# Splitting the streamed weights two blocks at a time in a TensorE-bound kernel of four model layers

## The chip, the cores and the metric

The kernel runs on one core of a Trainium2 chip. The metric is the device time of one execution in microseconds (us).

## The reference

Four transformer layers work on 256 tokens of width 2048, in float32. The first two have three mixers side by side (a causal depthwise convolution over 31 tokens, a gated linear recurrence with 6 heads, retention with 6 heads) and a feed-forward with squared ReLU of width 8192, each followed by a layer norm of the residual sum. The third has neighbourhood attention, a gated delta rule in both directions and attention on a memory; the fourth has differential attention and attention on the memory. Cut to what the time goes into:

```python
proj = einsum('btd,de->bte', x, w_in[l])              # 2048 x 7168
...                                                   # mixers on parts of proj
x = layer_norm(ALPHA * x + mix @ w_out[l], ...)       # 2048 x 2048
f = square(relu(x @ w_ff1[l]))                        # 2048 x 8192
x = layer_norm(ALPHA * x + f @ w_ff2[l], ...)         # 8192 x 2048
...                                                   # twice, then
h = rmsnorm(x, ln_g); proj = h @ w_in                 # and out: x + mix @ w_out, twice
```

The results have to be near float32, so each product is made of three: weights and activations are split into a high part, which TensorE takes as float32r, and the difference to it, the low part, and hi·hi + lo·hi + hi·lo is summed.

## The kernel before

**Units and blocks.** All large products run through one weight stream. A unit is 512 output columns of a weight matrix over 2048 rows; it has 8 blocks of 256 rows (BLOCKS = 8), each 128 partitions x 2 x 512 elements, 512 KB. There are 140 units, 1120 blocks. The program numbers blocks of a stage with c and keeps block c in ring buffer j = c % 8 of `raw` (as loaded), `w_hi` and `w_lo`; `w_lo` lies in the same memory as `raw`. `ps_unit` has two buffers of sums, for units in turn.

**The four engines of the stream.** SyncE (`sp_unit`, L243) waits with `block_done` until block c-8 has been used, then loads block c and raises `raw_ready[j]` by 16. ScalarE (`act_split`, L251) waits for `raw_ready[j]` and copies `raw` to `w_hi` (L255), raising `hi_ready` by 1. VectorE (`dve_split`, L258) waits for `hi_ready` and subtracts (L262), raising `lo_ready`. TensorE (`pe_block`, L265) waits for `lo_ready` to reach c + 1 and issues 12 matmuls (L279 to L281: 2 row groups x 2 token tiles x 3 products), the last of which raises `block_done`.

**Order around the splits.** Each engine runs a list of instructions written out by hand. ScalarE and VectorE are 6 blocks ahead of TensorE (AHEAD = 6): in the place that belongs to TensorE's block c they split block c + 6, and between those places stands their other work: taking sums out of `ps_unit` (L697, L712), the transposed activations (`act_turn_bank`, `dve_turn_bank`, L766 and L779), and the mixers. `split_units` (L624) is the plain loop, `Meanwhile` (L651) hands out splits one at a time between the mixers' steps, and `act_feed_forward` and `dve_feed_forward` have their own loops. In the very first unit of the program the six blocks 0 to 5 are split one by one between the first transposes (L3702, L3751).

**The seams.** Where a layer norm ends one stage and the next stage multiplies its result, the two are interleaved. TensorE (`pe_seam_last`, `pe_seam_first`) works through the last unit's second half token tile by token tile, so that the norm of tile 0 can start, and then takes the next unit: blocks 0 to 3 for tile 0, blocks 0 to 3 for tile 1, blocks 4 to 7 for both, with eight transposing steps (L307, four matmuls each, a bank of `ps_mix` per step) between them: banks 2 and 3 after blocks 2 and 3 of tile 0, 4 and 5 in tile 1, 6 and 7 after block 4. It waits for the low part of block 2 and of block 3 when it takes them for tile 0. ScalarE's part is `act_seam` (L353), VectorE's is `dve_seam` (L374): statistics of a tile, then `norm.columns` (for LayerNorm L438, a reciprocal L443, L446), which write x 512 columns at a time, `dve_seam_bank` (L371), the low part of a transposed bank, and at three places a split: block 3 (L408), and blocks 4 and 5 inside the loop of L412:

```python
    dve_split(dve, k, b0, c0 + SEAM - 1)
    norm.columns(dve, k, 1, (0, 1))
    dve_seam_bank(dve, k, 2)
    dve_seam_bank(dve, k, 3)
    for c in (2, 3):
        norm.columns(dve, k, None, (c,))
        dve_split(dve, k, b0, c0 + SEAM + c - 2)
        for t in range(TT):
            dve_seam_bank(dve, k, 2 * c + t)
```

There are four seams: two with layer norm in layer 1 (after w_out, and after the feed-forward), one in layer 2 (after w_out), and one with RMS norm between layers 3 and 4.

Of the kernel before, what the change touches and what calls it, by code (L numbers as in the profile page):

```python
# [7 lines left out]
F32 = mybir.dt.float32  # L8
F32R = mybir.dt.float32r
I32 = mybir.dt.int32  # L10
ACT = mybir.ActivationFunctionType
ALU = mybir.AluOpType
# [21 lines left out]
BLOCKS = 8  # L34
# [216 lines left out]
def act_split(act, k, b0, c):  # L251

    j = c % BLOCKS
    act.wait_ge(k.raw_ready[j], b0 * 2 + 16 * (c // BLOCKS + 1))
    k.nc.scalar.activation(k.w_hi[:, j], k.raw[:, j], ACT.Copy).then_inc(k.hi_ready, 1)  # L255


def dve_split(dve, k, b0, c):  # L258

    j = c % BLOCKS  # L260
    dve.wait_ge(k.hi_ready, b0 + (c + 1))
    k.nc.vector.tensor_tensor(k.w_lo[:, j], k.raw[:, j], k.w_hi[:, j].bitcast(F32), ALU.subtract).then_inc(k.lo_ready, 1)  # L262


def pe_block(pe, k, b0, c, hi, lo, tiles=range(TT), at=None):  # L265
# [358 lines left out]
def split_units(eng, k, who, split, units, take=None, last=False):  # L624


    first = k.block0[who]
    k.block0[who] += units * BLOCKS
    pairs = units // 2

    def pair(b0, i, ending):
        for s in range(2):
            for c in range(AHEAD, AHEAD + BLOCKS):
                if take and c == AHEAD + BLOCKS - 1:
                    take(b0, s, i)
                if not (ending and s == 1 and c >= BLOCKS):
                    split(eng, k, b0, s * BLOCKS + c)

    loops = pairs - 1 if last else pairs
    if loops:  # L640
        with eng.Fori(0, loops) as i:
            pair(i * (2 * BLOCKS) + first, i, False)
    if last:
        pair(first + loops * 2 * BLOCKS, loops, True)
# [49 lines left out]
def act_take_proj(act, k, column=0):  # L694
    def take(b0, s, i):
        wait_unit(act, k, b0, s)
        k.nc.scalar.activation(k.proj[:, :, bass.ds(i * (2 * NC) + (column + s * NC), NC)], k.ps_unit[:, s],  # L697
                               ACT.Copy).then_inc(k.evacuated, BLOCKS)
    return take
# [524 lines left out]
def act_conv(act, k, l, run):  # L1224

    a = k.nc.scalar
    act.wait_ge(*run.evacuated(0))
    cg = k.proj[:, :, CG:CG + CONV_C]
    a.activation(cg, cg, ACT.Sigmoid).then_inc(*k.conv_gate.up())
    run(28)  # L1230
    act_hgrn_gates(act, k, l, run)
    upto(run, 40 + LATE * l)
    act.wait_ge(*k.conv_var.next("act"))
    a.activation(k.conv_rstd[:], k.conv_mv[:, :, 1], ACT.Sqrt, bias=k.eps[:, 0:1]).then_inc(*k.conv_root.up())
    run(2)
    act.wait_ge(*k.conv_linear.next("act"))
    ca = k.proj[:, :, CA:CA + CONV_C]
    a.activation(ca, ca, ACT.Silu).then_inc(*k.conv_done.up())
# [478 lines left out]
def act_take_first(act, k):  # L1717


    take_proj = act_take_proj(act, k, HQ)  # L1720

    def take(b0, s, i):
        if HQ + (2 * i + s) * NC < RG_LAST:
            return take_proj(b0, s, i)
        wait_unit(act, k, b0, s)
        k.nc.scalar.activation(k.proj[:, :, RG_LAST:RG_LAST + NC], k.ps_unit[:, s], ACT.Silu).then_inc(k.evacuated, BLOCKS)
    return take
# [344 lines left out]
def act_gate_split(act, k):  # L2072
    act.wait_ge(*k.gw_in.next("act", 16))
    k.nc.scalar.activation(k.gw_hi[:], k.gw_raw[:], ACT.Copy).then_inc(*k.gw_hi_ready.up())
# [1549 lines left out]
def two_blocks_kernel(nc, dram, out):  # L3624
    k = set_up(nc, dram, out)
# [4 lines left out]
    with nc.Block() as block:  # L3630
# [69 lines left out]
        @block.scalar  # L3700
        def _(act):
            for c in range(AHEAD):  # L3702
                act_split(act, k, 0, c)
                act_turn_bank(act, k, c)
            for g in range(AHEAD, BLOCKS):
                act_turn_bank(act, k, g)
            act.wait_ge(*k.eps_set.next("act"))
            for l in range(DEPTH):
                split_units(act, k, "act", act_split, CONV_UNITS, act_take_proj(act, k))
                run = Meanwhile(act, k, "act", act_split, IN_UNITS - CONV_UNITS, act_take_first(act, k))  # L3710
                act_conv(act, k, l, run)
                if l == 0:
                    act_positions(act, k)
                act_hgrn(act, k, l, run)
                act_retention(act, k, l, run)
                act_out_units(act, k, act_ln_root(act, k), late={AHEAD + 1: (4,), AHEAD + 3: (5, 6, 7)})
                if l < DEPTH - 1:
                    act_feed_forward(act, k, l, root=act_ln_root(act, k))
                else:
                    act_feed_forward(act, k, l, between=act_memory(act, k))  # L3720

            run = Meanwhile(act, k, "act", act_split, MEM_UNITS, act_take_memory(act, k))
            run(1)
            act_layer_norm(act, k)
            run(10)
            act.wait_ge(*k.normed.next("act", BLOCKS))
            act_rms(act, k, k.x, k.normed_x)
            run(6)
            act_gate_split(act, k)
            run.rest()  # L3730
            act_turn(act, k)
            split_units(act, k, "act", act_split, DELTA_UNITS, act_take_proj(act, k, DQ))
            run = Meanwhile(act, k, "act", act_split, IN_UNITS - DELTA_UNITS, act_take_columns(act, k, EVEN_COLUMNS))
            act_even_inputs(act, k, run)
            act_even_attention(act, k)
            act_delta(act, k, run)
            act_out_units(act, k, act_rms_root(act, k))
            split_units(act, k, "act", act_split, IN_UNITS - ODD_UNITS, act_take_proj(act, k, MQ))
            act_odd_attention(act, k, Meanwhile(act, k, "act", act_split, ODD_UNITS, act_take_odd(act, k)))
            act_odd_out(act, k)  # L3740

        @block.vector
        def _(dve):
            dve.sem_inc(k.evacuated, 2 * BLOCKS)
            dve.sem_inc(k.f_lo_ready, 2)
            dve.wait_ge(*k.consts_in.next("dve", 16))
            for g in range(BLOCKS):
                if g % 2 == 0:
                    dve.wait_ge(*k.x_in[g // 2].next("dve", 16))
                    dve.sem_inc(*k.turn_source.up(2))  # L3750
                if g < AHEAD:  # L3751
                    dve_split(dve, k, 0, g)
                dve_turn_bank(dve, k, g)
            for l in range(DEPTH):
                split_units(dve, k, "dve", dve_split, CONV_UNITS)
                run = Meanwhile(dve, k, "dve", dve_split, IN_UNITS - CONV_UNITS)
                if l == 0:
                    dve_positions(dve, k)
                dve_conv(dve, k, l, run)
                dve_hgrn(dve, k, l, run)  # L3760
                dve_retention(dve, k, l, run)
                dve_out_units(dve, k, LayerNorm(ALPHA), late={AHEAD + 2: (5, 6, 7)})
                if l < DEPTH - 1:
                    dve_feed_forward(dve, k, l, norm=LayerNorm(None))
                else:
                    dve_feed_forward(dve, k, l, between=dve_memory(dve, k))
            run = Meanwhile(dve, k, "dve", dve_split, MEM_UNITS)
            dve_layer_norm(dve, k, FF_GROUPS * OUT_UNITS, k.normed, run)
            run(14 - run.done)
            dve.wait_ge(*k.row_in.next("dve", 16))  # L3770
            dve_rms(dve, k, k.x, k.normed_x, k.gain, run)
            run(20 - run.done)
            dve_gate_split(dve, k)
            run.rest()
            dve_turn(dve, k)
            split_units(dve, k, "dve", dve_split, DELTA_UNITS)
            dve_gate_rows(dve, k)
            run = Meanwhile(dve, k, "dve", dve_split, IN_UNITS - DELTA_UNITS)
            dve_even_inputs(dve, k, run)
            dve_even_attention(dve, k)  # L3780
            dve_delta(dve, k, run)
            dve_out_units(dve, k, RootMeanSquare())
            split_units(dve, k, "dve", dve_split, IN_UNITS - ODD_UNITS)
            dve_odd_attention(dve, k, Meanwhile(dve, k, "dve", dve_split, ODD_UNITS))
            dve_odd_out(dve, k)
# [57 lines left out]
```

## Time and profile before

| | |
|---|---|
| median of 3 runs | 3428.34 us (3423.22 to 3429.39) |
| the profiled execution, its own time | 3427.86 us |
| its span | 3426.1 us |
| TensorE (PE) busy | 3379.8 us, 99% |
| VectorE (DVE) busy | 2187.7 us, 64% |
| ScalarE (ACT) busy | 1592.4 us, 46% |
| high copies, L255 | 1120, 1174.4 us |
| low differences, L262 | 1120, 1373.6 us |
| mean granted TensorE clock | 0.999 |

The span is what the profiler saw of the execution from its first to its last instruction; busy times are unions over it. An instruction of VectorE or ScalarE begins a little before the one ahead of it ends, so start-to-start is shorter than the duration. Matmuls overlap too: one of 512 columns is shown as 0.39 us, and the next starts about 0.23 us after it.

### The profile page before, as it was taken

To read this page: it belongs to the slowest core of one execution; us is meant where nothing else is said; L and a number is where in the kernel's file an instruction comes from. 1 tells how busy PE (TensorE), PEld (TensorE's weight loads), DVE (VectorE), ACT (ScalarE), POOL (GpSimd) and SP (SyncE) were. 2 spreads that over 40 slices of the span, in tenths; PEclk is the share of its full clock that TensorE was granted. 3 is DMA by queue.
4 is the path that set the end of the run, shared out by engine and by line. 5 is a ranking of instruction groups with operands and counts; after the bars stand their busy time and mean duration, and the time that the engine had idled before them with its cause. 6 is when DMAs were issued, how large, how long until landed. Compare 5 with 4: busy or idle time off the path is not lost.

```text
span 3426.1 us, 42773 instructions
## 1 busy us (share of the span) xinstructions
PE 3379.8 (99%) x16007; PEld 2819.9 (82%) x16007; DVE 2187.7 (64%) x2543; ACT 1592.4 (46%) x1968; POOL 366.7 (11%) x394
## 2 busy tenths in 40 slices
PE   8999999999999999999999999999999999999999
PEld 7888878888888787888788888888888889888887
DVE  5976666555555678865665656667446676656664
ACT  4554444444434346444444444344445643365563
POOL 0035001010101001520101010100000152000100
PEclk9999999999999999999999999999999999999999
DMA  7645666666666665556767666766666701565644
GB/s 235 191 141 167 198 207 213 198 212 199 212 200 213 186 197 171 146 156 206 258 205 212 199 208 203 206 197 207 186 178 175 205 31 52 187 189 172 181 133 166
DMA packets 333642, 633.82 MB, mean 185 GB/s; under 512 B 27561, under 2 KB 37801, under 8 KB 331803
## 3 DMA queue, kind: packets, MB, share of 16 engines
q1 hardware_dynamic: 313120, 595.93, 57.4%
q0 software_dynamic: 11136, 29.18, 2.8%
q10 hardware_dynamic: 9216, 6.30, 0.6%
q8 instruction: 123, 2.02, 0.2%
q14 instruction: 47, 0.39, 0.0%
HBM read 612.44 MB, written 2.10 MB: 179 GB/s over the span
## 4 chain that ended last, share of the span: by engine, by line
PE 91%; DVE 4%; ACT 3%; DMA 1%; issue 1%; ACTq 0%; SPq 0%; DVEq 0%
PE ps_unit L279 28%; PE ps_unit L281 27%; PE ps_unit L280 27%; PE ps_mix L2980 2%; PE ps_mix L1362 1%; DVE sb_w_lo L262 1%; ACT sb_w_hi L255 1%; DMA sb_raw<-in_w_in_dram 1%; PE ps_mix L737 0%; PE ps_mix L307 0%; DVE sb_x L438 0%; DMA sb_raw<-in_w_ff_dram 0%; PE ps_mix L3410 0%; DMA sb_raw<-in_e_w_in_dram 0%; PE ps_mix L3430 0%
## 5 line engine op out<-in xcount | busy, mean ns | idle before, releaser
L262 DVE TENSOR_TENSOR sb_w_lo<-sb_raw,sb_w_hi 128x1024 fp32r<-128x1024 f32 x1120 | 1373.6, 1241 | 996.2 <-ACT sb_w_hi L255 990.9
L255 ACT ACTIVATE sb_w_hi<-sb_raw 128x1024 fp32r<-128x1024 f32 x1120 | 1174.4, 1059 | 1450.8 <-DMA sb_raw<-in_w_ff_dram 530.4
L279 PE MATMUL ps_unit<-sb_w_hi,sb_a_hi 128*128 128x512 f32 x3456 | 1360.5, 394 | 7.5 <-DVE sb_a_lo L779 4.8
L281 PE MATMUL ps_unit<-sb_w_hi,sb_a_lo 128*128 128x512 f32 x3456 | 1347.9, 390 | 0.0
L280 PE MATMUL ps_unit<-sb_w_lo,sb_a_hi 128*128 128x512 f32 x3456 | 1347.0, 390 | 0.0
L279 PEld LDWEIGHTS ps_unit<-sb_w_hi,sb_a_hi 128*128 128x128 f32 x3456 | 650.2, 188 | 144.7 <-DVE sb_a_lo L779 5.4
L281 PEld LDWEIGHTS ps_unit<-sb_w_hi,sb_a_lo 128*128 128x128 f32 x3456 | 649.9, 188 | 136.8
L280 PEld LDWEIGHTS ps_unit<-sb_w_lo,sb_a_hi 128*128 128x128 f32 x3456 | 650.6, 188 | 131.7
L279 PE MATMUL ps_unit<-sb_w_hi,sb_f_hi 128*128 128x512 f32 x1024 | 399.2, 390 | 0.0
L281 PE MATMUL ps_unit<-sb_w_hi,sb_f_lo 128*128 128x512 f32 x1024 | 398.5, 389 | 0.0
L280 PE MATMUL ps_unit<-sb_w_lo,sb_f_hi 128*128 128x512 f32 x1024 | 398.4, 389 | 0.0
L281 PEld LDWEIGHTS ps_unit<-sb_w_hi,sb_f_lo 128*128 128x128 f32 x1024 | 192.3, 188 | 40.1
L280 PEld LDWEIGHTS ps_unit<-sb_w_lo,sb_f_hi 128*128 128x128 f32 x1024 | 192.3, 188 | 39.6
L279 PEld LDWEIGHTS ps_unit<-sb_w_hi,sb_f_hi 128*128 128x128 f32 x1024 | 192.3, 188 | 39.6
L1000 POOL DMA_DIRECT2D sb_f_in<-sb_f_out x192 | 94.0, 497 | 1105.5 <-DVE sb_f_out L1053 1102.7
L1288 DVE SCALAR_TENSOR_TENSOR sb_conv_y<-sb_conv_u,sb_conv_w,sb_conv_y 128x255 f32<-128x255 f32 (+29 forms) x240 | 96.9, 474 | 0.1
L712 DVE TENSOR_TENSOR sb_x<-sb_x,ps_unit 128x1024 f32<-128x1024 f32 (+1 forms) x43 | 49.3, 1147 | 70.0 <-PE ps_unit L281 69.7
L697 ACT ACTIVATE sb_proj<-ps_unit 128x1024 f32<-128x1024 f32 (+1 forms) x45 | 46.1, 1025 | 79.0 <-PE ps_unit L281 79.0
L1454 POOL TENSOR_TENSOR sb_h_d<-sb_h_cum 128x768 f32<-128x768 f32 x16 | 37.1, 2318 | 339.0 <-DVE sb_h_cum L1525 251.8
L723 DVE BATCH_NORM_STATS2 sb_stats<-sb_x 128x6 f32<-128x512 f32 x80 | 51.5, 686 | 1.4
L975 ACT ACTIVATE sb_f_hi<-sb_f_out 128x512 fp32r<-128x512 f32 x64 | 36.9, 624 | 28.9 <-DVE sb_f_out L1024 28.7
L350 ACT ACTIVATE sb_a_hi<-ps_mix 128x512 fp32r<-128x512 f32 x32 | 18.7, 598 | 64.0 <-PE ps_mix L307 64.0
(474 smaller groups left out, 1972.5 us busy)
## 6 DMA issues: line engine op xcount, KB each, us to landing
sb_raw<-in_w_ff_dram SPq DMA_DIRECT2D x512, 512.0 KB, 3.8
sb_raw<-in_w_in_dram SPq DMA_DIRECT2D x224, 512.0 KB, 3.7
sb_raw<-in_e_w_in_dram SPq DMA_DIRECT2D x112, 512.0 KB, 3.5
sb_raw<-in_o_w_in_dram SPq DMA_DIRECT2D x112, 512.0 KB, 4.5
sb_raw<-in_w_out_dram SPq DMA_DIRECT2D x64, 512.0 KB, 4.0
sb_raw<-in_e_w_out_dram SPq DMA_DIRECT2D x32, 512.0 KB, 4.4
sb_raw<-in_o_w_out_dram SPq DMA_DIRECT2D x32, 512.0 KB, 3.6
sb_raw<-in_e_w_mem_kv_dram SPq DMA_DIRECT2D x16, 512.0 KB, 4.5
```

Source lines behind the costliest of these rows:

```text
L255: k.nc.scalar.activation(k.w_hi[:, j], k.raw[:, j], ACT.Copy).then_inc(k.hi_ready, 1)
L262: k.nc.vector.tensor_tensor(k.w_lo[:, j], k.raw[:, j], k.w_hi[:, j].bitcast(F32), ALU.subtract).then_inc(k.lo_ready, 1)
L279: k.nc.tensor.matmul(acc, hi[:, kt, tokens], w_hi, start=kt == 0, stop=False)
L280: k.nc.tensor.matmul(acc, hi[:, kt, tokens], w_lo, start=False, stop=False)
L281: last = k.nc.tensor.matmul(acc, lo[:, kt, tokens], w_hi, start=False, stop=kt == KT - 1)
L697: k.nc.scalar.activation(k.proj[:, :, bass.ds(i * (2 * NC) + (column + s * NC), NC)], k.ps_unit[:, s], ACT.Copy).then_inc(k.evacuated, BLOCKS)
L712: return k.nc.vector.tensor_tensor(x, x, out, ALU.add)
L723: last = k.nc.vector.bn_stats(k.stats[:, t, bass.ds(chunk, 1), :].rearrange("p c s -> p (c s)"), k.x[:, t, cols])
L1000: pool.dma_start(*moved_square(k, u, n)).then_inc(k.f_moved_pool[u % 2], 16)
L1288: ins = v.scalar_tensor_tensor(y, u, w, y, ALU.mult, ALU.add)
L1454: g.tensor_tensor(d[:, :, 0, :], middle, c[:, :, 0, :], ALU.subtract)
L2980: last = tensor.matmul(out[:, x, :], left(n), right[:, n, :], start=True, stop=True)
```

## The change

`act_split` and `dve_split` do nothing for an even buffer j. For an odd j they wait for both blocks, j-1 and j, and treat them in one instruction of 2048 elements per partition (the two ring buffers are next to each other), raising `hi_ready` and `lo_ready` by 2. So an even block is split in the place that belonged to the odd one behind it. The loops that call them are as before. The six single blocks at the start get functions of their own, which are the old ones. TensorE's and SyncE's programs are unchanged, and so are all numbers that are waited for.

```diff
 def act_split(act, k, b0, c):
 
     j = c % BLOCKS
+    if j % 2 == 0:
+        return
+    act.wait_ge(k.raw_ready[j - 1], b0 * 2 + 16 * (c // BLOCKS + 1))
     act.wait_ge(k.raw_ready[j], b0 * 2 + 16 * (c // BLOCKS + 1))
-    k.nc.scalar.activation(k.w_hi[:, j], k.raw[:, j], ACT.Copy).then_inc(k.hi_ready, 1)
+    k.nc.scalar.activation(k.w_hi[:, j - 1:j + 1], k.raw[:, j - 1:j + 1], ACT.Copy).then_inc(k.hi_ready, 2)
+
+
+def act_split_one(act, k, c):
+
+    act.wait_ge(k.raw_ready[c], 16)
+    k.nc.scalar.activation(k.w_hi[:, c], k.raw[:, c], ACT.Copy).then_inc(k.hi_ready, 1)
 
 
 def dve_split(dve, k, b0, c):
 
     j = c % BLOCKS
+    if j % 2 == 0:
+        return
+    pair = slice(j - 1, j + 1)
     dve.wait_ge(k.hi_ready, b0 + (c + 1))
-    k.nc.vector.tensor_tensor(k.w_lo[:, j], k.raw[:, j], k.w_hi[:, j].bitcast(F32), ALU.subtract).then_inc(k.lo_ready, 1)
+    k.nc.vector.tensor_tensor(k.w_lo[:, pair], k.raw[:, pair], k.w_hi[:, pair].bitcast(F32), ALU.subtract)\
+        .then_inc(k.lo_ready, 2)
+
+
+def dve_split_one(dve, k, c):
+
+    dve.wait_ge(k.hi_ready, c + 1)
+    k.nc.vector.tensor_tensor(k.w_lo[:, c], k.raw[:, c], k.w_hi[:, c].bitcast(F32), ALU.subtract).then_inc(k.lo_ready, 1)
...
             for c in range(AHEAD):
-                act_split(act, k, 0, c)
+                act_split_one(act, k, c)
                 act_turn_bank(act, k, c)
...
                 if g < AHEAD:
-                    dve_split(dve, k, 0, g)
+                    dve_split_one(dve, k, g)
                 dve_turn_bank(dve, k, g)
```

What moves in a seam, in the order of each engine's own instructions. VectorE in the first layer-norm seam, from the end of columns 2 on, before (L446 writes x, L262 is a split, L371 the low part of a bank, L438 the first half of columns 3):

```order
L446 SCALAR_TENSOR_TENSOR sb_x<-sb_x,sb_rstd,sb_shift 128x512 [waits dve_step]
L446 SCALAR_TENSOR_TENSOR sb_x<-sb_x,sb_rstd,sb_shift 128x512
L262 TENSOR_TENSOR sb_w_lo<-sb_raw,sb_w_hi 128x1024 [waits hi_ready]
L371 TENSOR_TENSOR sb_a_lo<-ps_mix,sb_a_hi 128x4x128 [waits turn_hi] x2
L438 SCALAR_TENSOR_TENSOR sb_x<-sb_x,sb_mv,sb_gain 128x512 [waits aggregated]
L438 SCALAR_TENSOR_TENSOR sb_x<-sb_x,sb_mv,sb_gain 128x512
L446 SCALAR_TENSOR_TENSOR sb_x<-sb_x,sb_rstd,sb_shift 128x512 [waits dve_step]
L446 SCALAR_TENSOR_TENSOR sb_x<-sb_x,sb_rstd,sb_shift 128x512
L262 TENSOR_TENSOR sb_w_lo<-sb_raw,sb_w_hi 128x1024 [waits hi_ready]
L371 TENSOR_TENSOR sb_a_lo<-ps_mix,sb_a_hi 128x4x128 [waits turn_hi] x2
```

and the same place in the changed kernel, whose lines have other numbers (L465 for L446, L390 for L371, L457 for L438, L274 for L262):

```order
L465 SCALAR_TENSOR_TENSOR sb_x<-sb_x,sb_rstd,sb_shift 128x512 [waits dve_step]
L465 SCALAR_TENSOR_TENSOR sb_x<-sb_x,sb_rstd,sb_shift 128x512
L390 TENSOR_TENSOR sb_a_lo<-ps_mix,sb_a_hi 128x4x128 [waits turn_hi] x2
L457 SCALAR_TENSOR_TENSOR sb_x<-sb_x,sb_mv,sb_gain 128x512 [waits aggregated]
L457 SCALAR_TENSOR_TENSOR sb_x<-sb_x,sb_mv,sb_gain 128x512
L465 SCALAR_TENSOR_TENSOR sb_x<-sb_x,sb_rstd,sb_shift 128x512 [waits dve_step]
L465 SCALAR_TENSOR_TENSOR sb_x<-sb_x,sb_rstd,sb_shift 128x512
L274 TENSOR_TENSOR sb_w_lo<-sb_raw,sb_w_hi 128x2048 [waits hi_ready]
L390 TENSOR_TENSOR sb_a_lo<-ps_mix,sb_a_hi 128x4x128 [waits turn_hi] x2
```

Block 4's split has moved from ahead of banks 4 and 5 and columns 3 to behind them.

ScalarE in the same seam, before (`turned` tells that TensorE has transposed a bank; `raw_ready4` is buffer 4's load):

```order
L350 ACTIVATE sb_a_hi<-ps_mix 128x4x128 [waits turned] x2
L255 ACTIVATE sb_w_hi<-sb_raw 128x1024 [waits raw_ready4]
L255 ACTIVATE sb_w_hi<-sb_raw 128x1024 [waits raw_ready5]
L350 ACTIVATE sb_a_hi<-ps_mix 128x4x128 [waits turned] x4
L255 ACTIVATE sb_w_hi<-sb_raw 128x1024 [waits raw_ready6]
L255 ACTIVATE sb_w_hi<-sb_raw 128x1024 [waits raw_ready7]
```

and now (L369 for L350, L258 for L255):

```order
L369 ACTIVATE sb_a_hi<-ps_mix 128x4x128 [waits turned] x2
L258 ACTIVATE sb_w_hi<-sb_raw 128x2048 [waits raw_ready5,raw_ready4]
L369 ACTIVATE sb_a_hi<-ps_mix 128x4x128 [waits turned] x4
L258 ACTIVATE sb_w_hi<-sb_raw 128x2048 [waits raw_ready7,raw_ready6]
L258 ACTIVATE sb_w_hi<-sb_raw 128x2048 [waits raw_ready1,raw_ready0]
```

Each pair stands where its two single copies stood together.

## Rows read from the trace of the kernel before

**Rows 1.** The page: busy time of each engine, share of the span, instructions.
```profile
PE 3379.8 (99%) x16007; PEld 2819.9 (82%) x16007; DVE 2187.7 (64%) x2543; ACT 1592.4 (46%) x1968; POOL 366.7 (11%) x394
```

**Rows 2.** Windows: stretch, then PE, PEld, DVE, ACT, POOL busy, clock, DMA, GB/s.
```profile
560.00:600.00 40.00, 40.00 (x178) 33.14 (x177) 21.52 (x21) 16.82 (x17) 2.93 (x6) 1.00 0.67 210
```

**Rows 3.** The page: loads of weight blocks, count, KB, us from issue to landing.
```profile
sb_raw<-in_w_ff_dram SPq DMA_DIRECT2D x512, 512.0 KB, 3.8
```

**Rows 4.** Groups by form: count, busy us, mean ns of one, idle before.
```profile
L262 DVE TENSOR_TENSOR sb_w_lo<-sb_raw,sb_w_hi 128x1024 fp32r<-128x1024 f32 x1120 | 1373.6, 1241 | 996.2 <-ACT sb_w_hi L255 990.9
L255 ACT ACTIVATE sb_w_hi<-sb_raw 128x1024 fp32r<-128x1024 f32 x1120 | 1174.4, 1059 | 1450.8 <-DMA sb_raw<-in_w_ff_dram 530.4 <-DMA sb_raw<-in_w_in_dram 257.0 <-issue 216.9
L1952 ACT ACTIVATE sb_normed_x<-sb_x 128x2048 f32<-128x2048 f32 x2 | 3.8, 1903 | 0.0
L2311 DVE TENSOR_TENSOR sb_proj<-sb_proj,sb_head_ss 128x1536 f32<-128x1536 f32 x8 | 13.9, 1755 | 0.1
```

**Rows 5.** Groups by form, TensorE: the transposes of the seams.
```profile
L307 PE MATMUL ps_mix<-sb_square,sb_x 128*128 128x128 f32 x96 | 14.4, 277 | 6.5 <-DVE sb_x L446 6.5
L307 PE MATMUL ps_mix<-sb_square,sb_normed_x 128*128 128x128 f32 x32 | 4.7, 274 | 0.2 <-DVE sb_normed_x L476 0.2
```

**Rows 6.** Timeline of VectorE, first seam: start us, us, instruction, idle before.
```profile
467.27 1.21 DVE L262 TENSOR_TENSOR sb_w_lo<-sb_raw,sb_w_hi 128x1024 fp32r<-128x1024 f32 x1
...
477.26 1.22 DVE L262 TENSOR_TENSOR sb_w_lo<-sb_raw,sb_w_hi 128x1024 fp32r<-128x1024 f32 x1
...
481.93 1.41 DVE L446 SCALAR_TENSOR_TENSOR sb_x<-sb_x,sb_rstd,sb_shift 128x512 f32<-128x512 f32 x2
483.26 1.22 DVE L262 TENSOR_TENSOR sb_w_lo<-sb_raw,sb_w_hi 128x1024 fp32r<-128x1024 f32 x1
...
486.20 8.04 DVE L262 TENSOR_TENSOR sb_w_lo<-sb_raw,sb_w_hi 128x1024 fp32r<-128x1024 f32 x7
```

**Rows 7.** Timeline of ScalarE, first seam: the splits from block 6 on.
```profile
485.11 6.75 ACT L255 ACTIVATE sb_w_hi<-sb_raw 128x1024 fp32r<-128x1024 f32 x7
```

**Rows 8.** Timeline of TensorE, first seam: transposes, first matmuls of blocks 4, 5, 6.
```profile
470.73 0.66 PE L307 MATMUL ps_mix<-sb_square,sb_x 128*128 128x128 f32 x4 [1.19 <-DVE sb_x L446]
...
480.62 0.50 PE L279 MATMUL ps_unit<-sb_w_hi,sb_a_hi 128*128 128x512 f32 x1
...
484.53 0.50 PE L279 MATMUL ps_unit<-sb_w_hi,sb_a_hi 128*128 128x512 f32 x1
...
487.58 0.47 PE L279 MATMUL ps_unit<-sb_w_hi,sb_a_hi 128*128 128x512 f32 x1
```

**Rows 9.** Waits of TensorE: waited for, us in total, times, longest.
```profile
PE ps_mix L3418 <- DVE sb_o_att_e L3539: 3.2, 1, 3.2
...
PE ps_mix L1642 <- DVE sb_r_rstd L1737: 2.8, 2, 1.7
PE ps_mix L1263 <- DVE sb_conv_y L1288: 2.4, 1, 2.4
PE ps_unit L279 <- DVE sb_w_lo L262: 1.8, 4, 0.9
...
PE ps_mix L1371 <- DVE sb_h_s L1550: 1.4, 1, 1.4
```

**Rows 10.** Windows of 1 us after two waits: TensorE busy, granted clock.
```profile
171.00:172.00 1.00, 1.00 (x4) 0.66 0.07 18
172.00:173.00 1.00, 1.00 (x4) 0.50 0.00 0
...
174.00:175.00 1.00, 1.00 (x4) 0.63 0.00 0
...
3317.00:3318.00 1.00, 1.00 (x7) 1.00 0.02 8
```

**Rows 11.** Timeline of VectorE: splits in the mixers.
```profile
167.08 1.23 DVE L262 TENSOR_TENSOR sb_w_lo<-sb_raw,sb_w_hi 128x1024 fp32r<-128x1024 f32 x1 [1.03 <-ACT sb_w_hi L255]
...
2905.57 2.36 DVE L262 TENSOR_TENSOR sb_w_lo<-sb_raw,sb_w_hi 128x1024 fp32r<-128x1024 f32 x2
...
3313.72 1.23 DVE L262 TENSOR_TENSOR sb_w_lo<-sb_raw,sb_w_hi 128x1024 fp32r<-128x1024 f32 x1 [4.06 <-ACT sb_w_hi L255]
```

## The prediction

> **What bounds the kernel now.** I read the page's busy times first: TensorE is busy 3379.8 of 3426.1 us, so 46.3 us are idle; VectorE is busy 64% of the span, ScalarE 46% [rows 1]. Less work on those two is worth at most what TensorE waits for them. Then the windows: in 40 us of feed-forward TensorE issues 178 matmuls of 512 columns [rows 2]; a block has 12, so it takes one block each 40 / 178 x 12 = 2.70 us.
>
> Then the weight ring. Eight buffers; the load of block c starts when block c-8 is done, so the load, ScalarE's high copy and VectorE's low difference must be through in 7 blocks, 18.9 us. Now they take 3.8 us [rows 3] + 1.06 + 1.24 [rows 4] = 6.1 us. 12.8 us are to spare, and TensorE's own waits name the low half with 1.8 us in all [rows 9]. The exceptions are the seams: the places where a layer norm's last tile is finished while TensorE already works on the next unit. There both splits stand between steps of the norm, and the timelines of one seam (467 to 488 us) are the second thing to read [rows 6 to 8].
>
> **The change in the steady ring.** 1120 blocks less 6 single ones make 557 pairs. ScalarE: its row of 2048 elements takes 1.90 us [rows 4], against 1.06 for 1024. VectorE: 1024 elements 1.24, 1536 elements 1.755 us [rows 4], hence about 1.03 us per 1024 more than what one takes: a pair takes about 2.29 us. The seven back to back splits start (8.04 - 1.22) / 6 = 1.137 us apart [rows 6], so a pair frees 2 x 1.137 - 2.205 = 0.07 us of VectorE, 39 us in all, none of it on TensorE's path. The pair waits for the second load, one block later: 2.7 + 3.8 + 1.90 + 2.29 = 10.7 us of 18.9. 8.2 us remain: cost nothing, as long as a load lands in under 12 us.
>
> The Trainium skill says more for the change: "VectorE: DVE Perf Modes", section on the TRN2 errata, has every instruction pay a fixed latency between instructions, once for a large tile and again for each small one; by its figure of about 151 cycles at 0.96 GHz a pair would save 157 ns, 88 us over 557 pairs (an estimate by that page). The splits of [rows 6] overlap by 0.085 us, so the trace gives less than half of that.
>
> **The seams.** There are four: 96 + 32 transposes at L307, 32 each [rows 5]. In each the even block of a pair loses its own place and gets that of the odd one, while TensorE takes it as early as before. Numbers of the first seam; blocks 2 to 7 of the unit:
> - Pair 2+3, in the place of block 3's split, 467.27 us [rows 6]: VectorE is 2.205 - 1.137 = 1.07 us longer, and the columns of x behind it, for which TensorE waits 1.19 us before its transposes at 470.73 [rows 8], come 1.07 us later. **+1.07**. With no slack there all behind it moves.
> - Pair 4+5. Block 4 was split at 477.26, block 5 at 483.26 [rows 6]. The pair stands at 483.26. The 1.14 us that leave at 477.26 don't help: the next two low halves wait for TensorE's transposes. So 483.26 + 1.07 + 2.29 = 486.62, and TensorE begins block 4 at 486.67 where it began at 480.62 [rows 8]: +6.05, or **+4.98** on top. The pause is about 5 us.
> - Pair 6+7. After block 4 come the transposes of the last two banks; ScalarE copies them out and right behind that splits block 6, at 485.11 [rows 7]. This chain follows block 4, so the pair begins at 485.11 + 6.05 = 491.16, its high copy ends at 493.06, its low half at 493.09 + 2.29 = 495.38, TensorE's matmul follows 0.16 us behind it, as now, at 495.54 instead of 487.58 [rows 8]: +7.96, **+1.9** on top. Block 5 follows block 4 by 3.91 us (484.53 less 480.62 [rows 8]), begins at 490.58 and is done 2.6 us later, so a second pause of 2.3 us stands before block 6.
> Later blocks have 3 us and more to spare. Sum 7.95 us a seam; 4 x 7.95 = **+31.8 us**. (The RMS seam has other steps of the same length.) Bounds: 1.07 + 4.98 alone, if the last chain hides (24 us), to 9 us each (36).
>
> **The clock.** Pauses of this length can cost twice. After the wait of 2.4 us for sb_conv_y the windows show a granted clock of 0.50, that is 1.2 GHz, with 4 matmuls a us in place of 6, from 171.3 to 174.7 us (0.66 and 0.63 in the slices at its ends); after the wait of 3.2 us for sb_o_att_e it stays at 1.00, 2.4 GHz [rows 9, 10]. The slow stretch of 3.4 us costs half of that, 1.7 us. The changed seam has a pause of 5 us and one of 2.3 us in a row; I take one stretch a seam: 4 x 1.7 = **+6.8 us**, bounds 0 and 13.6. [...] Of the waits in the rows one had the fall and one not, so the sum keeps 6.8.
>
> **The mixers.** Where VectorE had an even split, waiting for ScalarE, just ahead of a step that TensorE waits for, that split is gone. At 167.08 us the split waited 1.03 us and took 1.23 [rows 11] ahead of the last taps: the 2.4 us wait shrinks by some 1.2 (the pair before costs 1 us), and its slow stretch goes, 1.7. At 3313.72 the split of an even block waited 4.06 us [rows 11] ahead of sb_o_att_e: 3.0 of the 3.2 us go. The waits for sb_h_s (1.4) and sb_r_rstd (2.8, two times) [rows 9] have an even split ahead as well: 4.0 of their 4.2. Sum -10.9. On the other side, where TensorE takes an even block just after its split: at 2905.57 both splits follow each other [rows 11] with TensorE taking the first 0.12 us after it, so a pair costs (1.90 - 1.06) + (2.29 - 1.22) = 1.9 us; I count seven more places where a pair falls in front of TensorE's next need, each bounded by 0 and 2 us, and take 1.3 each: 9.1. Net **+0.1**, bounds -9 and +8.
>
> **Sum.** The profiled execution has 3427.86 us (span 3426.1, 1.8 around it), 0.5 below the median of 3428.34. 3427.9 + 31.8 + 6.8 + 0.1 = **3466.6 us**, 1.1% slower.
>
> **Rivals.**
> - The clock holds in the seams. For it: it held after 3.2 us [rows 9, 10]. 3459.8 us.
> - The clock falls at every pause, two stretches a seam, 6.8 us more. For it: the fall after only 2.4 us [rows 9, 10]. 3473.4 us. [...]
> - Everything is paid: two slow stretches a seam (+6.8 more) and the mixers' losses whole (+8). For it: there is hardly an idle us on TensorE that could hide them. 3466.6 + 14.8 = 3481.
> - The ring hides the seams too. For it: 8.2 us of slack for a pair. Against it: what binds there is the place in VectorE's order, not the load. 3428, no change.
> - Faster: the even splits that vanish ahead of steps TensorE waits for give 10.9 us, and the seam costs little. It decides where a seam costs less than 10.9 / 4 = 2.7 us, and would give 3417 if it cost nothing. Against it: the pair 4+5 can't be earlier than the columns ahead of it in VectorE's order.
> - The fixed cost of an instruction reaches TensorE. If VectorE bound the two convolutions, where an estimated 40 blocks each pass, 20 pairs x 0.07 x 2 = 2.8 us would come back: 3425 us. For it: the wait for sb_conv_y [rows 9]. Against it: VectorE itself waits for ScalarE there, at 167.08 [rows 11]. The Trainium skill's page on VectorE (its section on the errata, above) would have it so, with more per pair.
>
> **Chances.** Forecast 0.45, clock holds 0.20, falls at every pause 0.12, all paid 0.15, hidden 0.03, faster by vanished splits 0.03, by fixed cost 0.02. A difference under 0.2%, 7 us, is about what a measurement of this kernel can tell from no change, and the rival at 3425 falls within it. So faster 0.03, same 0.05, slower 0.92. The range takes in the case without clock falls with the mixers at their better half, and the case with all paid: 3452 to 3482 us.
>
> **What would show it.** L262's successor with 2048 elements: near 2.29 us and x557; ScalarE's near 1.90. TensorE's waits name sb_w_lo with 4 x (5 + 2) us, some 28 us, where 1.8 stood; its idle sum rises from 46 to some 75. In a seam the columns at 481.93 come 1.07 us later, block 4 starts right behind the pair, block 6 about 8.8 us after block 4 (6.9 before). Windows of 1 us behind the 5 us pause show 0.50 or 1.00. The waits for sb_o_att_e and sb_h_s are gone. I am wrong if TensorE's wait for sb_w_lo stays under 10 us, if a pair takes much over 2.4 us, or if landing times rise to 8 us, which would be loads that collide.

## The result, and the profile after

The changed kernel takes 3497.56 us in the median (4 runs, 3495.29 to 3499.38), the kernel before in the same series 3426.14 (4 runs). The ratio is 1.0208, with a 95% interval of 1.0198 to 1.0223: 2.1% slower, 71 us. Forecast were 39 us and at most 54, so the sign is right and the size is not. The profiled execution has a span of 3495.3 us, 69.2 more than before. Its rows, first the page's busy times and the forms of the splits, then TensorE's waits:

```profile
PE 3404.9 (97%) x16007; PEld 2830.7 (81%) x16007; DVE 2106.8 (60%) x1986; ACT 1489.7 (43%) x1411; POOL 363.1 (10%) x394
...
L274 DVE TENSOR_TENSOR sb_w_lo<-sb_raw,sb_w_hi 128x2048 fp32r<-128x2048 f32 x557 | 1288.3, 2321 | 1056.9 <-ACT sb_w_hi L258 1054.7
L258 ACT ACTIVATE sb_w_hi<-sb_raw 128x2048 fp32r<-128x2048 f32 x557 | 1061.3, 1915 | 1465.8 <-DMA sb_raw<-in_w_ff_dram 475.7
...
sb_raw<-in_w_ff_dram SPq DMA_DIRECT2D x512, 512.0 KB, 4.0
```

```profile
PE ps_unit L298 <- DVE sb_w_lo L274: 52.9, 30, 5.1
PE ps_mix L1381 <- DVE sb_h_s L1572: 6.8, 8, 1.8
...
PE ps_mix L326 <- DVE sb_x L465: 4.4, 9, 0.8
```

Against [rows 1] VectorE is 81 us less busy and ScalarE 103, and none of it is in the time. TensorE's idle time rose from 46.3 to 3495.3 - 3404.9 = 90.4 us, and its busy time by 25.1 us for the same 16007 matmuls. So 44 us of the loss are waiting. Of the 25, the half clock takes 21: windows lose 24.5 us while TensorE is busy, against 3.4 before. The last 4 are, by an estimate, waiting too: a matmul is shown for 0.39 us and the next starts 0.23 us after it, so each pause begins 0.16 us earlier than the idle time shows, and there are 27 more of them. Forecast were about 33.6 (31.8 + 0.1, and 1.7 of the mixers' gain that was clock) and 5.1 (6.8 - 1.7).

The waits for sb_w_lo, 1.8 us in [rows 9], are 52.9 in 30 places: 34.5 in the seams, where 28 were forecast, 10.2 in the feed-forward, where none was, and 8.3 in front of three blocks in the mixers (3.96, 2.29, 2.02). The waits for sb_conv_y, sb_r_rstd and sb_o_att_e are gone from their places of [rows 9]; one of 0.7 us for sb_o_att_e stands at another block. The wait for sb_h_s of [rows 9], 1.4 us at L1371, is gone too. The trace of before has another one, at L1362, which is L1381 now:

```profile
PE ps_mix L1362 <- DVE sb_h_s L1553: 2.9, 2, 2.0
```

That one grew from 2.9 us in 2 places to 6.8 in 8.

The first seam, TensorE (start us, us, instruction, idle before) and VectorE:

```profile
482.64 0.77 PE L298 MATMUL ps_unit<-sb_w_hi,sb_a_hi 128*128 128x512 f32 x1 [5.08 <-DVE sb_w_lo L274]
...
489.02 0.48 PE L298 MATMUL ps_unit<-sb_w_hi,sb_a_hi 128*128 128x512 f32 x1
...
494.30 0.47 PE L298 MATMUL ps_unit<-sb_w_hi,sb_a_hi 128*128 128x512 f32 x1 [2.30 <-DVE sb_w_lo L274]
```
```profile
478.88 1.42 DVE L465 SCALAR_TENSOR_TENSOR sb_x<-sb_x,sb_rstd,sb_shift 128x512 f32<-128x512 f32 x2
480.21 2.28 DVE L274 TENSOR_TENSOR sb_w_lo<-sb_raw,sb_w_hi 128x2048 fp32r<-128x2048 f32 x1
489.50 1.29 DVE L390 TENSOR_TENSOR sb_a_lo<-ps_mix,sb_a_hi 128x512 fp32r<-128x512 f32 x2 [7.00 <-ACT sb_a_hi L369]
491.86 6.70 DVE L274 TENSOR_TENSOR sb_w_lo<-sb_raw,sb_w_hi 128x2048 fp32r<-128x2048 f32 x3 [1.07 <-ACT sb_w_hi L258]
```

The pauses are those of the forecast: 5.08 us in front of block 4, which starts right behind its pair, and 2.30 us in front of block 6, at 494.30. What differs is the granted clock. Windows of 1 us of the same place (stretch, then PE, PEld, DVE, ACT, POOL busy, clock, DMA, GB/s):

```profile
480.00:481.00 1.00, 0.00 (x0) 0.00 (x0) 1.00 (x2) 0.00 (x0) 0.00 (x0) 1.00 0.91 332
481.00:482.00 1.00, 0.00 (x0) 0.00 (x0) 1.00 (x1) 0.00 (x0) 0.00 (x0) 0.87 0.28 107
482.00:483.00 1.00, 0.36 (x1) 0.39 (x2) 0.49 (x1) 0.00 (x0) 0.00 (x0) 0.50 0.00 0
...
487.00:488.00 1.00, 1.00 (x4) 0.66 (x3) 0.00 (x0) 0.00 (x0) 0.00 (x0) 0.50 0.00 0
488.00:489.00 1.00, 1.00 (x9) 1.00 (x8) 0.00 (x0) 0.13 (x1) 0.00 (x0) 0.71 0.00 0
...
494.00:495.00 1.00, 0.70 (x3) 0.65 (x4) 1.00 (x2) 1.00 (x1) 0.00 (x0) 1.00 0.94 369
495.00:496.00 1.00, 1.00 (x4) 0.78 (x4) 1.00 (x1) 0.35 (x1) 0.00 (x0) 0.70 0.99 393
```

Half clock (1.2 GHz) begins inside the 5 us pause and lasts to 488.6, 6.8 us; a second stretch of 3.4 us follows the 2.3 us pause. Windows over the whole span, the missing part of the clock times their length added up, lose 27.4 us in this execution and 3.4 in that of before. The part that lies in a pause, here from 481.7 to 482.6, costs nothing.

The other loss is where the forecast had written nothing: inside the feed-forward. Four rows of VectorE, then SyncE's and ScalarE's DMA issues and the pair behind them, one unit of layer 2:

```profile
1746.21 1.31 DVE L1072 STREAM_TRANSPOSE sb_f_out<-ps_unit 128x512 f32<-128x512 f32 x2
...
1762.60 1.22 DVE L1043 SCALAR_TENSOR_TENSOR sb_f_out<-sb_f_in 128x1024 f32<-128x1024 f32 x1
...
1766.91 4.49 DVE L274 TENSOR_TENSOR sb_w_lo<-sb_raw,sb_w_hi 128x2048 fp32r<-128x2048 f32 x2 [0.58 <-ACT sb_w_hi L258]
1771.32 1.31 DVE L1072 STREAM_TRANSPOSE sb_f_out<-ps_unit 128x512 f32<-128x512 f32 x2
```
```profile
1772.66 2.75 SPq L931 DMA_DIRECT2D sb_f_in<-sb_f_out  x4
1775.67 5.38 SPq L938 DMA_DIRECT2D sb_raw<-in_w_ff_dram  x6
```
```profile
1772.66 3.74 ACTq L999 DMA_DIRECT2D sb_f_in<-sb_f_out  x6
1776.53 1.92 ACT L258 ACTIVATE sb_w_hi<-sb_raw 128x2048 fp32r<-128x2048 f32 x1 [7.91 <-issue]
1781.34 1.92 ACT L258 ACTIVATE sb_w_hi<-sb_raw 128x2048 fp32r<-128x2048 f32 x1 [2.90 <-DMA sb_raw<-in_w_ff_dram]
```

VectorE reads a unit's sums out of PSUM (L1072) behind the pairs 10+11 and 12+13. Only then can SyncE issue the four squares' moves and ScalarE its six; the next weight loads stand behind the four, the next pair's high copy behind the six, and the next L1072 behind all of these. That is a loop, here 1771.32 - 1746.21 = 25.1 us round; the other rounds of both layers take 22.5 to 25.3. TensorE's own unit takes 21.8 us, from the starts of its blocks in the kernel before (21.6 by [rows 2]). The loop runs only through the first four units of each group of eight; behind them the splits regain their lead, and a group loses time only where its slow rounds use that lead up, most in the first group behind a seam. Taken by place, from TensorE's starts of blocks, after against before, the 69.2 us are 50.0 in the four seams (12.5, 12.7, 11.9, 12.9), 15.4 in the feed-forward (3.7 in layer 1, 11.7 in layer 2) and 3.8 in all the rest.

### The profile page after: what moved, and what is told of

It reads as the page before. It is cut to its first block and busy times, and to the rows that moved or that the text cites. A ratio compares the mean times of both kernels' runs of the same rounds, so it can differ in the third digit from the quotient of the medians.

```text
span 3495.3 us, 42525 instructions
## 1 busy us (share of the span) xinstructions
PE 3404.9 (97%) x16007; PEld 2830.7 (81%) x16007; DVE 2106.8 (60%) x1986; ACT 1489.7 (43%) x1411; POOL 363.1 (10%) x394
## 3 DMA queue, kind: packets, MB, share of 16 engines
q8 instruction: 123, 2.02, 0.2%
## 5 line engine op out<-in xcount | busy, mean ns | idle before, releaser
L274 DVE TENSOR_TENSOR sb_w_lo<-sb_raw,sb_w_hi 128x2048 fp32r<-128x2048 f32 x557 | 1288.3, 2321 | 1056.9 <-ACT sb_w_hi L258 1054.7
L258 ACT ACTIVATE sb_w_hi<-sb_raw 128x2048 fp32r<-128x2048 f32 x557 | 1061.3, 1915 | 1465.8 <-DMA sb_raw<-in_w_ff_dram 475.7
L298 PE MATMUL ps_unit<-sb_w_hi,sb_a_hi 128*128 128x512 f32 x3456 | 1369.0, 396 | 53.8 <-DVE sb_w_lo L274 46.3
L298 PEld LDWEIGHTS ps_unit<-sb_w_hi,sb_a_hi 128*128 128x128 f32 x3456 | 654.5, 189 | 196.5 <-issue 46.3
L1061 DVE TENSOR_TENSOR sb_f_lo<-sb_f_out,sb_f_hi 128x512 fp32r<-128x512 f32 x64 | 41.4, 689 | 37.7 <-ACT sb_f_hi L994 37.7
L369 ACT ACTIVATE sb_a_hi<-ps_mix 128x512 fp32r<-128x512 f32 x32 | 18.7, 597 | 100.0 <-PE ps_mix L326 100.0
```

Source lines behind the costliest of these rows:

```text
L258: k.nc.scalar.activation(k.w_hi[:, j - 1:j + 1], k.raw[:, j - 1:j + 1], ACT.Copy).then_inc(k.hi_ready, 2)
L274: k.nc.vector.tensor_tensor(k.w_lo[:, pair], k.raw[:, pair], k.w_hi[:, pair].bitcast(F32), ALU.subtract)\
L298: k.nc.tensor.matmul(acc, hi[:, kt, tokens], w_hi, start=kt == 0, stop=False)
L1061: last = k.nc.vector.tensor_tensor(feature_tokens(k.f_lo, u - 1, t), feature_rows(k, u - 1, t), feature_tokens(k.f_hi, u - 1, t).bitcast(F ...
```

## The experiments

All are made from one kernel in which each call of the two helpers asks a rule how to split: its block alone ("one"), the pair at the odd block's call ("late", as the change) or the pair at the even block's ("early"). The first six blocks are always single. Places are "ff" (the calls in the feed-forward), "seam23" and "seam45" (the calls for blocks 2 to 5 of a seam) and "mix" (the rest). A seam's 6+7 lies in "ff" at the first and third seam, and in "mix" at the other two. The diffs show the rule against the change's ("late" everywhere); the line numbers differ by up to some twenty from the changed kernel's. Ratios are to the kernel before on the same chip, whose median was 3424 to 3425.5.

**Pairs only in the feed-forward.**
```diff
-    return "late"
+    return "late" if place == "ff" else "one"
```


> Pairs only in the two feed-forward layers; the seams and the mixers keep single splits. Theory (a loop in the feed-forward: VectorE's sums of a unit stand behind the pairs 10+11 and 12+13, the squares' DMAs and the loads queued behind them start after the sums, and the next pair waits for those loads): about +15 us, 3441, with TensorE waiting for sb_w_lo some 10 to 15 us inside units and the landing time still near 4 us. Rival 1, the stalls in the feed-forward are only echoes of the late seams: 3426 to 3429. Rival 2, loads collide: also slower, but with a landing time of the feed-forward loads of 5 us and more.

3447.55 us, ratio 1.0066 (1.0053 to 1.0080), some 23 us slower. The median landing time is 3.9 us, so loads don't collide, and nothing late came from outside: the feed-forward slows down by itself. It is more than expected. The 6+7 of two seams is a pair here: TensorE's blocks 6 come 2.0 us later at both, and one of them has a slow stretch, 5.6 us together in the profile, beside 16.1 inside the two feed-forwards. Another 2.8 us are half clock behind the wait for sb_o_att_e, which in the kernel before was as long and brought none.

**Pairs only for 2+3 and 4+5 of the seams.**
```diff
+    return "late" if place in ("seam23", "seam45") else "one"
```


> Pairs only for blocks 2+3 and 4+5 at the four seams, single splits everywhere else, 6+7 too. Theory (each seam pays 1.07 + 4.98 us of waiting and a slow stretch of nearly 7 us, which costs 3.4): 4 x 9.5 = +38 us, 3464. Rival, the long slow stretch comes only with both pauses together: 4 x (6.05 + 1.7) = +31 us, 3457. Rival, the clock plays no part and the excess was waiting: 4 x 6.05 = +24 us, 3450, with a granted clock of 1.00 behind the pause.

3456.68 us, ratio 1.0095 (1.0079 to 1.0110). The time is that of the first rival, but not for its reason. The idle time rose by 67.0 - 46.3 = 20.7 us, the clock's loss by 13.6, a part of it in the pauses: the seams have one, two, two and three stretches of 3.4 us, not one each. The same pause of 5.08 us is followed by one stretch in the first seam and by two in the second (the same columns as above):

```profile
481.00:482.00 1.00, 0.54 (x1) 0.50 (x2) 0.31 (x1) 0.00 (x0) 0.00 (x0) 0.53 0.00 0
...
484.00:485.00 1.00, 1.00 (x4) 0.78 (x4) 0.00 (x0) 0.00 (x0) 0.00 (x0) 0.76 0.00 0
485.00:486.00 1.00, 1.00 (x7) 0.80 (x6) 0.00 (x0) 0.00 (x0) 0.00 (x0) 1.00 0.00 0
...
1191.00:1192.00 1.00, 0.00 (x0) 0.00 (x0) 1.00 (x1) 0.00 (x0) 0.00 (x0) 0.52 0.38 143
...
1197.00:1198.00 1.00, 1.00 (x4) 0.65 (x4) 0.00 (x0) 0.00 (x0) 0.00 (x0) 0.57 0.00 0
```

**Pairs everywhere else.**
```diff
+    return "late" if place == "mix" else "one"
```


> Pairs everywhere but in the feed-forward and for 2+3 and 4+5 of the seams; 6+7 of a seam is a pair here. Theory: pair 6+7 costs about 1.9 us a seam and may bring a slow stretch worth 1.7, so 8 to 14 us, and the mixers alone give about +4: 3438 to 3445. Rival, the forecast's mixers (net 0) with 6+7 hidden behind single splits of 4 and 5: 3426 to 3430.

3438.17 us, ratio 1.0043 (1.0029 to 1.0057). The time is the expected one, but in part by luck: four seams had been counted, and 6+7 is a pair here in two of them. By TensorE's starts those two cost 5.6 us with one slow stretch, and layer 3 costs 3.9. The three runs share no pair and hold all 557, and they add up: 23.5 + 32.7 + 14.2 = 70.4 us against the change's 71.

**Every pair in the even block's place.**
```diff
+    return "one" if place == "start" else "early"
```


> Every pair of the change, but taken in the even block's place on both engines and not in the odd one's. Theory (the loss is the even block's lost place, not the size of the instruction): the 5 us pause before block 4 and its slow stretch are gone, the sums of the feed-forward come earlier; what is left is 1.1 us per seam step and waits for the second load: 3425 to 3440. Rival 1, a pair of 2.29 us is itself too coarse for this order: 3460 and more. Rival 2, the saved fixed costs reach TensorE: under 3419.

3566.62 us, ratio 1.0422 (1.0408 to 1.0436): the theory fell as a rule for the whole kernel, and the time is in the range of Rival 1. Where the theory had been taken from it held: in the seams the step of 5 us before block 4 is gone, and each costs 1.5 to 2.6 us. But the mixers pay more than all the rest did: of the 130 us that the profile is longer, 118 lie outside the seams and the feed-forward. TensorE's waits there:

```profile
PE ps_mix L3438 <- DVE sb_o_att_e L3559: 15.7, 3, 9.2
...
PE ps_mix L1382 <- DVE sb_h_s L1573: 11.8, 9, 2.6
PE ps_mix L1662 <- DVE sb_r_rstd L1757: 10.0, 2, 5.2
PE ps_mix L1344 <- ACT sb_proj L1439: 9.4, 2, 4.8
```

Placed early, ScalarE's pair waits for the odd block's load (loads of w_in alone: 334 us of waiting in place of 257), and the step of the mixer behind it waits too.

**All three pairs of a seam.**
```diff
+    return "late" if place in ("seam23", "seam45") or (place == "ff" and c in (6, 7)) or g in (406, 407, 982, 983) else "one"
```
(`g` is the block's number in the program.)

> Pairs only at the seams, for 2+3, 4+5 and now 6+7 as well (6+7 of a group's first unit in all groups of the feed-forward, where the ring has room). Theory (half clock comes in stretches of 3.4 us that lose 1.7 each; with pauses of 5.1 and 2.3 us in a row three of them fall in a seam, 5.1 us): waiting 4 x 8 and clock 4 x 5.1, less what the mixers catch up: about +48 us, 3472, that is 15 above the run with 2+3 and 4+5 alone. Rival, the clock falls as often as in that run (13.7 us in all) and 6+7 adds its 2 us of waiting only: +41 us, 3465.

3471.91 us, ratio 1.0131 (1.0113 to 1.0149). The theory's number, but partly by luck. In the profile the idle time is 29.2 us above that of before, and the clock's loss 22.2 us, of which 15.4 in the seams: 9 stretches of 3.4 us, three in two of the seams, two in one and one in another, where the theory had three in each. The runs of this kernel spread by 14 us, those of most others by 3 to 7 and only those of the run with every pair early by more (16).

**Feed-forward without the buffers 6 and 7.**
```diff
+    return "late" if place == "ff" and j < 6 else "one"
```


> Pairs only in the feed-forward and there only for the buffers 0 to 5; 6+7 stay single, so the seams have no pair. Theory (VectorE's sums stand behind the pairs of the buffers 2 to 5, the loads behind the squares feed the pair of the buffers 0 and 1): the whole feed-forward loss stays, +13 to +17 us, 3437 to 3441, and the clock is lost nowhere in the feed-forward. Rival, pair 6+7 is a part of the loop: under +8 us, below 3432.

3446.30 us, ratio 1.0056 (1.0042 to 1.0070). The loss stays, and no clock is lost (3.4 us, as before), so the loop doesn't need the pair 6+7. But 20.8 us are more than the theory had: by TensorE's starts 21.0 lie inside the two feed-forwards, against 16.1 with pairs for 6+7 as well, and why fewer pairs cost more there is not shown. TensorE now waits 0.7 to 0.8 us in front of block 2, in twelve units of the two layers.

**The change, with the sums ahead of pair 12+13.**
```diff
             for j in range(AHEAD + 4, AHEAD + 8):
...
+                if u < 4 and j == AHEAD + 7:
+                    wait_unit(dve, k, b0, u)
...
+                    last.then_inc(k.evacuated, BLOCKS)
                 dve_split(dve, k, b0, u * BLOCKS + j)
...
-            if u < 4:
-                wait_unit(dve, k, b0, u)
...
-                last.then_inc(k.evacuated, BLOCKS)
```


> The change as it is, but VectorE takes the sums of a feed-forward unit ahead of the pair 12+13 and not behind it. Theory (the loop through the sums is what slows the feed-forward): 10 to 15 us come back, 3483 to 3488, and TensorE's waits for sb_w_lo inside units are gone. Rival 1, the load is late for another reason (the squares' DMAs collide with the weights): no change, 3496 to 3499. Rival 2, the pair behind the sums is now itself late for TensorE: slower than 3499.

3479.49 us, ratio 1.0158 (1.0144 to 1.0172): 18 us come back. By TensorE's starts some 15 of them lie inside the two feed-forwards, where the changed kernel's loss is gone whole; elsewhere the clock loses 3.4 us less. VectorE takes the sums every 21.8 us now, as TensorE makes them; in the same part of layer 2, after a round of 24.4 us, it catches up with one of 20.6:

```profile
1714.01 1.30 DVE L1063 STREAM_TRANSPOSE sb_f_out<-ps_unit 128x512 f32<-128x512 f32 x2
1715.24 2.25 DVE L282 TENSOR_TENSOR sb_w_lo<-sb_raw,sb_w_hi 128x2048 fp32r<-128x2048 f32 x1
...
1734.58 1.30 DVE L1063 STREAM_TRANSPOSE sb_f_out<-ps_unit 128x512 f32<-128x512 f32 x2
```

**One pair a seam, 4+5, in block 4's place.**
```diff
+    return "early" if place == "seam45" else "one"
```


> One pair a seam, 4+5, made in block 4's place and not in block 5's; everything else single. Theory (the 5 us pause comes from the place, not from the size): the steps behind come 1.1 us later or not even that, no slow clock in the seams: 3424 to 3430. Rival, a 2.29 us instruction anywhere in the seam delays TensorE in full or the pair must wait for block 5's load: 2 to 5 us a seam, 3434 to 3445.

3425.13 us, ratio 1.0000 (0.9991 to 1.0009): nothing. The same instruction of 2.29 us costs 5 us and slow clocks in block 5's place and nothing in block 4's. VectorE, first seam:

```profile
472.81 1.42 DVE L467 SCALAR_TENSOR_TENSOR sb_x<-sb_x,sb_rstd,sb_shift 128x512 f32<-128x512 f32 x2
474.14 2.29 DVE L282 TENSOR_TENSOR sb_w_lo<-sb_raw,sb_w_hi 128x2048 fp32r<-128x2048 f32 x1
476.35 1.28 DVE L392 TENSOR_TENSOR sb_a_lo<-ps_mix,sb_a_hi 128x512 fp32r<-128x512 f32 x2
```

**Four pairs, where the even split had been in the way.**
```diff
+    return "late" if g // 2 * 2 in (56, 58, 1088, 1090) else "one"
```


> Single splits everywhere, but pairs for the blocks 56 to 59 and 1088 to 1091, where the even split stood ahead of a step that TensorE waits for (the convolution's last taps, the last attention's output). Theory (there the vanished even split is a gain): the wait for sb_conv_y shrinks from 2.4 to under 1.5 us and its slow stretch goes, 3 to 5 us, the wait for sb_o_att_e of 3.2 us goes: 3416 to 3420. Rival, the time comes back at the next step that TensorE needs: 3423 to 3426.

3417.45 us, ratio 0.9979 (0.9970 to 0.9988). Faster than the kernel before. TensorE's start of block 1084 gains 3.4 us at once and those of 54 and 55 gain 4.2; the slow stretch at 171 us [rows 10] is gone. So is the other one of the kernel before, at 1355.8 us, though the pause of 2.4 us ahead of it is still there: that 1.7 us is chance and not the change's.

**Two pairs more.**
```diff
+    return "late" if g // 2 * 2 in (56, 58, 98, 502, 1088, 1090) else "one"
```


> The run with pairs for 56 to 59 and 1088 to 1091 and two pairs more, 98+99 and 502+503, whose even split stood ahead of the steps that give sb_r_rstd. Theory (a vanished even split ahead of a step that TensorE waits for is a gain): TensorE's waits for sb_r_rstd, 2.8 us, go, so 1.5 to 3 us less than that run: 3414 to 3416. Rival, these waits move to the next step: no difference, 3417 to 3418.

3414.08 us, ratio 0.9971 (0.9960 to 0.9983). No wait for sb_r_rstd is left, and TensorE's starts behind the two places come 1.3 and 1.9 us earlier. The intervals of this run and the one before overlap, so the times alone don't show the step from four pairs to six. With six pairs in place of 557 the change's idea makes the kernel 10 us faster.

**The change, mended.** The sums ahead of 12+13 as above, and
```diff
+    if place == "seam45":
+        return "early"
+    if place in ("start", "seam23") or (place == "ff" and c in (6, 7)) or g in (406, 407, 950, 951, 982, 983):
+        return "one"
     return "late"
```


> The change with its three found faults mended: pair 4+5 of a seam in block 4's place, 2+3 and 6+7 of the seams and 950+951 single, the sums of a feed-forward unit ahead of the pair 12+13. Theory: of the 54 us that are left with the sums first, the seams' 32 of waiting and 20 of clock go but for about 4, the mixers stay about even: 3425 to 3436. Rival, the mixers pay more once the seams no longer hide it: 3437 to 3445. Rival, the saved fixed costs of 540 instructions reach TensorE: under 3418.

3433.04 us, ratio 1.0029 (1.0018 to 1.0040). Of 71 us some 62 are gone. The seams are as fast as before, to 0.2 us each. What is left can be placed by TensorE's starts. Three blocks wait longer than before for their low half, 456 and 1058 in the mixers and 558 at the head of layer 2's feed-forward (the last three rows are ScalarE's copy for block 558 and, in the same stretch, a load of GpSimd's and the weight loads):

```profile
PE ps_unit L304 <- DVE sb_w_lo L286: 11.3, 8, 4.1
...
1331.46 0.47 PE L304 MATMUL ps_unit<-sb_w_hi,sb_a_hi 128*128 128x512 f32 x1 [4.07 <-DVE sb_w_lo L286]
...
1672.24 0.50 PE L304 MATMUL ps_unit<-sb_w_hi,sb_a_hi 128*128 128x512 f32 x1 [3.70 <-DVE sb_w_lo L286]
...
1667.88 1.91 ACT L277 ACTIVATE sb_w_hi<-sb_raw 128x2048 fp32r<-128x2048 f32 x1 [5.07 <-DMA sb_raw<-in_w_ff_dram]
...
sb_mem<-in_mem_dram POOLq DMA_DIRECT2D x1, 2048.0 KB, 15.7
sb_raw<-in_w_ff_dram SPq DMA_DIRECT2D x4, 512.0 KB, 13.7
```

Block 456 comes 3.8 us later and brings a slow stretch: its single high copy stood ahead of a step of the mixer on ScalarE, and the pair stands behind it. Block 558 comes 3.6 us later, with a slow stretch as well. There GpSimd loads the memory input, and three weight loads around 1650 us land after 12 to 16 us and not 4; in the kernel before they took 11.9 to 14.2 and cost TensorE nothing, but a pair waits for the later of two. Block 1058 comes 2.2 us later, and the waits for sb_h_s are 7.0 us in 8 places. The vanished even splits give a part back. The page's busy row, with 50.9 us of idle time on TensorE:

```profile
PE 3379.0 (99%) x16007; PEld 2818.8 (82%) x16007; DVE 2111.5 (62%) x2001; ACT 1497.0 (44%) x1426; POOL 363.6 (11%) x394
```

VectorE has 76 us less to do than in [rows 1], ScalarE 95, and the kernel is slower.

## Why the prediction was wrong

- **The sign and the bound: right.** TensorE sets the time, and work taken from the other two buys nothing; a pair is 2.29 us (mean 2.32) and 1.92 us as worked out.
- **The walk through the seam: right.** The first two steps of the first seam came as +1.07 and +5.07, and block 6 has its pause of 2.30 us; the fourth seam, of the RMS norm, has pauses of 1.84, 3.63 and 2.31 us and came to nearly the same sum. TensorE is idle 31.6 us longer in the four seams than before, where 31.8 were forecast. (A pair was worked out as 2.29 us; the forecast's own terms, 1.24 + 1.03, give 2.27.) That block 4 loses its place is the cause: the pair in block 4's place costs nothing. The forecast's own reason against a gain, that the pair can't be ahead of the columns in VectorE's order, was true only for the place that the change chose.
- **The term "one slow stretch a seam": mis-sized.** Forecast was +6.8 us with bounds 0 and 13.6. The profiled execution has 13 stretches of 3.4 us in the four seams, three or four in each; some of it lies in the pauses. The seams took 50.0 us in place of 31.8 + 6.8, and as the pauses are the forecast's, the 11.4 more are clock: 18 us and not 7. Windows lose 22.2 us in the seams, 19.7 of them while TensorE is busy. The rows of before had shown one stretch after one pause, and I took that for the most that a pause can bring; a pause of 5 us brought one or two, and the 2.3 us behind it one more in the change. The rival "falls at every pause" was nearer, and its 13.6 too few as well.
- **The term "the steady ring costs nothing": failed, and it is the step that failed in kind.** Its 8.2 us of slack were reckoned for a ring in which a load starts when a block is done. In units 1 to 4 of each group of eight in the feed-forward this isn't so: SyncE's loads stand behind the squares, these behind VectorE's sums, and the sums behind two pairs. The loads still land in 4.0 us in the median, so the sign that I had named for an error (landing at 8 us) could not show it. It costs 15.4 us in the change, and as much came back when the sums were moved.
- **The mixers: near in sum, and that by luck.** Forecast was +0.1 net; its gains of 1.2, 1.7, 3.0 and 4.0 us add up to 9.9 and not 10.9, so by its own parts it was +1.1, and the whole forecast 3467.6. Measured is +3.8 outside the seams and the feed-forward, with three slow stretches there and two before. That, the seams' 11.4 and the feed-forward's 15.4 make up the miss of 30.5 us in the profiled executions. The gains came, some larger than worked out: blocks 54 and 55 start 3.9 us earlier, block 1084 3.4, and those behind sb_r_rstd 1.3 and 1.9; the wait for sb_h_s of [rows 9] is gone. So did +2.0 at the pair behind 2905.57. The losses went past their bound of 2 us a place: the pair of blocks 456 and 457, which ScalarE now copies behind a step of the mixer where it had copied 456 ahead of it, costs 3.7 us and, by half clock behind its pause of 3.96 us, 2.4 more. And the other wait for sb_h_s, which the forecast had not counted, grew by 3.9 us.
- **The fixed cost of an instruction: right to leave out.** The mended change has 542 pairs, so it pays this cost 542 times less on each of the two engines, and is slower than the kernel before by 9 us.

Open: what decides whether a pause is followed by half clock, and for how long. It is not the pause's place or length alone, as the last section shows, so single slow stretches, 1.7 us each, can't be charged to the pair in front of them. Open too: why the feed-forward without the pairs 6+7 loses more than with them.

## What to carry over

Slack in a ring of buffers is counted along every queue that a load or a copy stands in, not from the buffer's release alone: look for whatever the issuing engine waits for ahead of it, follow that round until it closes, and compare the loop's time with the bound engine's. Merging two instructions is first a question of which of the two places the merged one takes. Where the first one stood ahead of a step that the bound engine waits for, dropping it is the gain; where the bound engine takes the first one's result at once, it is the loss; so merge by place, six pairs here and not 557.

## What the runs showed of the hardware

Every slow stretch of the thirteen profiles, by the granted clock of their windows, was 3.4 us of half clock (1.2 GHz) or two or three times that, but for those that the end of the span cuts; 3.4 us of it cost 1.7. The windows lose 3.4 us in before (two stretches), 27.4 in the change, none with four pairs, 0.5 at the very end with six, 42.6 with all pairs early.

The same pause is not always followed by the same clock. A pause of 5.08 us in front of block 4 stands in four of the kernels, in three seams each. All twelve were followed by half clock, nine for 6.8 us and three for 3.4. The pause of 3.2 us for sb_o_att_e stands in six profiles, in each in front of the same instruction. In the kernel before and in the feed-forward run without the buffers 6 and 7 full clock followed; in four others it was half clock for 6.8 us. One of the four, with one early pair a seam (PE, PEld, DVE, ACT, POOL busy, clock, DMA, GB/s):

```profile
3311.70 1.11 PE L3439 MATMUL ps_mix<-sb_square,sb_o_att_e 128*128 128x128 f32 x4 [3.20 <-DVE sb_o_att_e L3560]
...
3312.00:3313.00 1.00, 1.00 (x5) 0.94 (x4) 0.78 (x1) 0.15 (x1) 0.00 (x0) 0.50 0.00 0
```

Shorter pauses fell both ways as well. Those of 2.3 us in front of block 6 were followed by half clock in all four seams of the change, one of 2.29 us that ends at 2961.3 us of the same execution was not, and the same one in the run with pairs everywhere else, at 2910.5 us, was. So the fall that the forecast took from the kernel before, and the one that it saw missing there, were each one draw of several. The Trainium skill, "TensorE: Matmul & The Clock Gate", section on HAM oscillation, tells of a kernel whose waits for DMA of about 3 to 5 us are each followed by the lower clock; the twelve pauses of 5.08 us agree with it, of the six of 3.2 us only four.
